# The convolution's input projection in wide pairs, with part of its elementwise work moved to ScalarE and GpSimd

## What is computed

```python
def short_conv_mixer(h, w_in, conv_w, w_out):
    """y = W_out( B * conv_w3( C * u ) ), [B, C, u] = W_in h; causal depthwise conv."""
    b_gate, c_gate, u = jnp.split(h @ w_in, 3, axis=-1)
    v = c_gate * u
    vp = jnp.pad(v, ((0, 0), (CONV_WIDTH - 1, 0), (0, 0)))
    conv = sum(conv_w[k] * vp[:, k:k + S] for k in range(CONV_WIDTH))
    return (b_gate * conv) @ w_out
```

## Time and profile before

| | us |
|---|---|
| median of 3 runs | 1196.76 (1193.81 to 1199.23) |
| the profiled execution | 1195.6 |
| its span, first to last instruction | 1193.8 |
| outside the span | 1.8 |
| TensorE busy | 1184.0, 99% |
| VectorE busy | 859.2, 72% |
| ScalarE busy | 644.1, 54% |
| GpSimd busy | 226.9, 19% |
| mean granted TensorE clock | 0.997 of full |

### The profile page before, as it was taken

The page is one execution under the profiler, slowest core; times in us unless marked ns, Lnnn a source line. Parts: engine busy times, 40 slices in busy tenths (PEclk is TensorE's granted clock), DMA queues, the critical chain, the costliest instruction groups (busy, mean ns, idle before and its releaser), DMA issues.

```text
span 1193.8 us, 19183 instructions
## 1 busy us (share of the span) xinstructions
PE 1184.0 (99%) x7641; PEld 1055.1 (88%) x7641; DVE 859.2 (72%) x1178; ACT 644.1 (54%) x860; POOL 226.9 (19%) x115
## 2 busy tenths in 40 slices
PE   9999999999999999999999999999999999999997
PEld 6888889988899888888999988888899978888886
DVE  6877767788868877766788786656578777766353
ACT  6655454465655755544643455444446784555432
POOL 1443301000000334310000024520000250455001
PEclk9999999999999999999999999999999999999999
DMA  8655555953245554555545555555576305555550
GB/s 319 212 180 198 186 177 187 275 209 107 106 151 180 178 208 177 194 194 182 177 161 186 187 204 206 179 197 192 181 278 233 121 19 177 186 202 178 184 202 36
DMA packets 31567, 218.03 MB, mean 183 GB/s; under 512 B 3584, under 2 KB 3856, under 8 KB 6272
## 3 DMA queue, kind: packets, MB, share of 16 engines
q1 hardware_dynamic: 29712, 210.07, 50.2%
q0 software_dynamic: 1488, 6.05, 1.8%
q10 hardware_dynamic: 288, 0.79, 0.2%
HBM read 215.82 MB, written 4.22 MB: 184 GB/s over the span
## 4 chain that ended last, share of the span: by engine, by line
PE 93%; DVE 4%; DMA 2%; ACT 1%; issue 1%; SPq 0%; DVEq 0%; ACTq 0%
PE bank L1634 38%; PE bank L1635 19%; PE bank L1627 7%; PE bank L1628 7%; PE bank L1629 7%; PE bank L1826 2%; PE bank L1825 2%; PE bank L1824 2%; DVE w_hl L858 1%; DMA raw<-weights 1%; PE bank L2081 1%; ACT w_hl L438 1%; PE bank L1975 0%; DMA par<-small 0%; PE bank L1755 0%
## 5 line engine op out<-in xcount | busy, mean ns | idle before, releaser
L858 DVE TENSOR_TENSOR w_hl<-raw,w_hl 128x2048 fp32r<-128x2048 f32 x194 | 444.0, 2289 | 134.1 <-ACT w_hl L438 133.2
L438 ACT ACTIVATE w_hl<-raw 128x2048 fp32r<-128x2048 f32 x195 | 370.5, 1902 | 135.8 <-PE bank L1635 46.6
L1634 PE MATMUL bank<-x_hl,w_hl 128*128 128x512 f32 x905 | 315.2, 394 | 0.2 <-DVE w_hl L1077 0.2
L377 POOL TENSOR_TENSOR hidden<-hid_f,hidden 128x256 fp32r<-128x256 f32 (+1 forms) x76 | 189.6, 2494 | 517.7 <-ACT hidden L521 306.0
L1635 PE MATMUL bank<-x_hl,w_hl 128*128 128x256 f32 x905 | 251.9, 278 | 0.0
L1634 PE MATMUL bank<-hidden,w_hl 128*128 128x512 f32 x608 | 210.9, 393 | 0.0
L1634 PEld LDWEIGHTS bank<-x_hl,w_hl 128*128 128x128 f32 x905 | 169.6, 187 | 39.1 <-DVE x_hl L908 0.7
L1635 PEld LDWEIGHTS bank<-x_hl,w_hl 128*128 128x128 f32 x905 | 170.4, 188 | 0.2
L1635 PE MATMUL bank<-hidden,w_hl 128*128 128x256 f32 x608 | 169.0, 278 | 0.0
L1634 PE MATMUL bank<-y_hl,w_hl 128*128 128x512 f32 x445 | 155.3, 395 | 0.0
L1627 PE MATMUL bank<-x_hl,w_hl 128*128 128x256 f32 x528 | 151.2, 286 | 0.1
(11 more groups left out here) (397 smaller groups left out, 1713.6 us busy)
## 6 DMA issues: line engine op xcount, KB each, us to landing
raw<-weights SPq DMA_DIRECT2D x197, 1024.0 KB, 4.9
bias_skew<-bias_rows POOLq DMA_DIRECT2D x1, 3072.0 KB, 28.6
gate_or_bias<-bias_skew POOLq DMA_DIRECT2D x1, 2048.0 KB, 10.3
h<-x_t SPq DMA_DIRECT2D x2, 512.0 KB, 5.6
con<-consts SPq DMA_DIRECT2D x1, 769.5 KB, 12.7
raw<-weights ACTq DMA_DIRECT2D x1, 512.0 KB, 5.1
raw<-weights SPq DMA_DIRECT2D x1, 512.0 KB, 7.5
sv<-last_gain POOLq DMA_DIRECT2D x1, 512.0 KB, 4.0
```

The lines of the kernel that those rows point to most:

```text
L377: nc.gpsimd.tensor_tensor(hidden[:, at, 1, :], src, hidden[:, at, 0, :].bitcast(F32), ALU.subtract).then_inc(hid_lo, 1)
L438: nc.scalar.activation(dst, src, ACT.Copy).then_inc(hi_split, 1)
L858: V.tensor_tensor(w_lo[:, s, :], raw[:, s, :], w_hi[:, s, :].bitcast(F32), ALU.subtract).then_inc(lo_split, 1)
L1634: mm(out_, w_hi[:, s, c:c + m], x, start=start, stop=False, **kw)
```

## The change

The product of conv_in is now done by `wide`, chunk j of a turn on banks 0 and 1, 2 and 3, or 4 and 5 (one bank for each tile of 128 features). ScalarE copies the second halves of both banks to SBUF (`conv_half`), VectorE adds the first halves to them (`whole`, into t_ab) and goes on from t_ab. The factor of the norm, which VectorE multiplied to B, is multiplied to the sum of the taps by GpSimd, as soon as the last tap is there. The low part of y is made by GpSimd too. VectorE's y_f waits for GpSimd's product (`taps_scaled`). In conv_out, the one place where a low product stood ahead of the wide one is now in the plain order; in conv_in, where there was none, one is added.

```diff
--- before.py
+++ after.py
@@ -93,6 +93,7 @@
 
 ACC, TURN, SUMS = 0, 4, 7
 OUT_BANKS = ((0, 1), (2, 1), (6, 1), (0, 0))
+CONV_BANKS = ((0, 1), (2, 1), (4, 1))
 NSA_OUT_BANKS = ((3, 1), (6, 1), (0, 1), (2, 0))
 HID = {"ffn1": 0, "ffn2": FF, "mlp0": 2 * FF, "mlp1": 2 * FF + MF}
 UPS = {"ffn1": FF, "ffn2": FF, "mlp0": MF, "mlp1": MF}
@@ -213,6 +214,7 @@
         dve_step, act_step = sem("dve_step"), sem("act_step")
         ab_ready, sum_ready, r_ready, rt_mm, conv_full = (
             sem("ab_ready"), sem("sum_ready"), sem("r_ready"), sem("rt_mm"), sem("conv_full"))
+        conv_second, taps_done, taps_scaled = sem("conv_second"), sem("taps_done"), sem("taps_scaled")
         rope_ang, rope_sin = sem("rope_ang"), sem("rope_sin")
         sv_done, qk_raw, ss_head = sem("sv_done"), sem("qk_raw"), sem("ss_head")
         rq_mm, rq_done = sem("rq_mm"), sem("rq_done")
@@ -393,6 +395,12 @@
             pool.dma_start(heads[:, 0:2, :], p_t).then_inc(p_in, 16)
             pool.wait_ge(p_in, 16)
             low("ffn2")
+            for i in range(4):
+                pool.wait_ge(taps_done, i + 1)
+                nc.gpsimd.tensor_tensor(hid_f[:, :, :], hid_f[:, :, :], r_two, ALU.mult).then_inc(taps_scaled, 1)
+                pool.wait_ge(op_hi, PC["conv"] + i + 1)
+                nc.gpsimd.tensor_tensor(y_l[:, 2 * i:2 * i + 2, :], y_f[:, 2 * i:2 * i + 2, :],
+                                        y_h[:, 2 * i:2 * i + 2, :].bitcast(F32), ALU.subtract).then_inc(op_lo, 1)
             low("mlp0")
             pool.wait_ge(chunk_used, C["mlp0"] + 2 * MF)
 
@@ -720,13 +728,24 @@
             nxt(PLE_GATE[3])
             nc.scalar.preload_act_table_set("natural_log_exp_and_others")
             c0 = C["conv_in"]
+
+            def conv_half(i, j):
+                act.wait_ge(chunk_used, i * 3 + (c0 + j + 1))
+                if j != 1:
+                    act.wait_ge(drained, i * 3 + (DRAIN["conv"] + j // 2))
+                nc.scalar.activation(second[:, j % 2, :, :], halves(CONV_BANKS[j], 1), ACT.Copy).then_inc(conv_second, 1)
+
+            conv_half(0, 0)
             nxt(c0)
             rsqrt("mix0", load=False)
 
             def conv_turn(i):
                 if not isinstance(i, int):
+                    conv_half(i, 0)
                     nxt_in(c0, 0, i, 3)
+                conv_half(i, 1)
                 nxt_in(c0, 1, i, 3)
+                conv_half(i, 2)
                 act.wait_ge(conv_full, i + 1)
                 nc.scalar.activation(y_h[:, bass.ds(i * 2, 2), :], y_f[:, bass.ds(i * 2, 2), :], ACT.Copy).then_inc(op_hi, 1)
                 nxt_in(c0, 2, i, 3)
@@ -1316,39 +1335,43 @@
 
             def conv_turn(i):
 
-                st.n = i * 8 + n
+                def whole(j):
+                    dve.wait_ge(conv_second, i * 3 + (j + 1))
+                    V.tensor_tensor(t_ab[:, :, :], halves(CONV_BANKS[j], 0), second[:, j % 2, :, :],
+                                    ALU.add).then_inc(drained, 1)
+                    dve.wait_ge(drained, i * 3 + (DRAIN["conv"] + j + 1))
+
+                st.n = i * 9 + n
                 for j in range(2):
-                    dve.wait_ge(chunk_used, i * 3 + (c0 + j + 1))
-                    st.done(V.tensor_tensor(t_ab[:, j, :], bank[:, TURN + j, 0:S], t_m[:, :], ALU.mult))
-                    V.tensor_tensor(v_pad[:, j, 2:S + 2], t_ab[:, j, :], bank[:, TURN + j, S:2 * S],
-                                    ALU.mult).then_inc(drained, 1)
-                    dve.wait_ge(drained, i * 3 + (DRAIN["conv"] + j + 1))
+                    whole(j)
+                    st.done(V.tensor_tensor(t_ab[:, 0, :], t_ab[:, 0, :], t_m[:, :], ALU.mult))
+                    st.done(V.tensor_tensor(v_pad[:, j, 2:S + 2], t_ab[:, 0, :], t_ab[:, 1, :], ALU.mult))
                     for k in range(3):
                         tap = 2 - k
                         w = par[:, bass.ds(i * 2 + (SM["conv_w"] + 8 * tap + j), 1)]
                         src = v_pad[:, j, tap:tap + S]
                         if k == 0:
                             st.done(V.tensor_scalar(hid_f[:, j, :], src, w, None, ALU.mult))
+                            continue
+                        ins = V.scalar_tensor_tensor(out=hid_f[:, j, :], in0=src, scalar=w, in1=hid_f[:, j, :],
+                                                     op0=ALU.mult, op1=ALU.add)
+                        if j == 1 and k == 2:
+                            ins.then_inc(taps_done, 1)
                         else:
-                            st.done(V.scalar_tensor_tensor(out=hid_f[:, j, :], in0=src, scalar=w,
-                                                           in1=hid_f[:, j, :], op0=ALU.mult, op1=ALU.add))
+                            st.done(ins)
                     if j == 1 or not isinstance(i, int):
                         nxt_in(c0, j, i, 3)
-                dve.wait_ge(chunk_used, i * 3 + (c0 + 3))
-                V.tensor_tensor(t_ab[:, :, :], two(bank[:, TURN + 2, :]), r_two, ALU.mult).then_inc(drained, 1)
-                dve.wait_ge(drained, i * 3 + (DRAIN["conv"] + 3))
+                whole(2)
+                dve.wait_ge(taps_scaled, i + 1)
                 V.tensor_tensor(y_f[:, bass.ds(i * 2, 2), :], t_ab[:, :, :], hid_f[:, :, :],
                                 ALU.mult).then_inc(conv_full, 1)
-                dve.wait_ge(op_hi, i + (PC["conv"] + 1))
-                V.tensor_tensor(y_l[:, bass.ds(i * 2, 2), :], y_f[:, bass.ds(i * 2, 2), :],
-                                y_h[:, bass.ds(i * 2, 2), :].bitcast(F32), ALU.subtract).then_inc(op_lo, 1)
                 nxt_in(c0, 2, i, 3)
 
 
             conv_turn(0)
             with dve.Fori(1, 4) as i:
                 conv_turn(i)
-            st.n = n + 32
+            st.n = n + 36
             made[0] += 4
 
             project_out("conv_out", "mlp0", x_h, x_l)
@@ -1694,7 +1717,7 @@
                                 pe.wait_ge(op_lo, PC[pieces] + p + 1)
                             for t in range(2):
                                 for k in range(KT // n * p, KT // n * (p + 1)):
-                                    if j == 0 and t == 0 and k == 1 and banks[j][1] > 0:
+                                    if j == 0 and t == 0 and k == 1 and pieces != "conv":
                                         last = wide_low_first(bank[:, banks[j][0], :], c % RING, 256, P, x[:, 1, :, :])
                                         continue
                                     last = out_tile(banks[j], (c + j) % RING, t, k, x, k == 0, k == KT - 1)
@@ -2037,14 +2060,14 @@
 
 
             c = C["conv_in"]
-            two_pairs(c, ((TURN, 0), (TURN + 1, 0)), x_hl, "mix0", 3, between=lambda: sum_squares(7))
+            two_pairs(c, CONV_BANKS, x_hl, "mix0", 3, between=lambda: sum_squares(7))
             arrived(c + 3)
-            pair((c + 2) % RING, TURN + 2, x_hl).then_inc(chunk_used, 1)
+            out_chunk(CONV_BANKS[2], (c + 2) % RING, x_hl)
             with pe.Fori(1, 4) as i:
                 for j in range(3):
                     arrived(i * 3 + (c + j + 1))
                     pe.wait_ge(drained, i * 3 + (DRAIN["conv"] + j - 2))
-                    pair((c + j) % RING, TURN + j, x_hl).then_inc(chunk_used, 1)
+                    out_chunk(CONV_BANKS[j], (c + j) % RING, x_hl)
             c = C["conv_out"]
             two_pairs(c, OUT_BANKS, y_hl, "conv", 3)
             for j in range(2, 4):
```

## The result

| | before | after |
|---|---|---|
| median, us | 1196.72 (11 runs) | 1203.2 (11 runs) |
| ratio of the runs | | 1.0054 [1.0042, 1.0066] |
| a second set beside the experiments | 1197.64 (26 runs) | 1203.49 (9 runs), 1.0050 [1.0031, 1.0069] |
| span of the profiled execution | 1193.8 | 1203.5 |
| conv_in's first matmul to mlp0's first, "stage time" below | 92.31 | 97.66 |

What follows compares the result with a forecast made beforehand. VectorE's turn of 18.3 takes the bound from TensorE's 16.65: splits slip +1.46, +0.57, 1.89 a loop turn, to +7.21 at chunk 13; TensorE starts it +5.4 later, giving 1202.2, range 1198.5 to 1206.3.

Steps and rivals of the forecast that it cites:

- VectorE is only 0.9 faster than TensorE, and it starts late: In conv_in before the change: VectorE's turn takes 16.42, TensorE's 17.28, and TensorE starts chunk 5 only 0.13 after its split.
- Sum of halves: New VectorE work in conv_in for j = 0 and 1: +1.44 a turn, upper bound +1.66; for j = 2 zero.
- the last tap no longer holds up the split: On VectorE in conv_in, gives back 0.05 in the first turn and about 0.1 in the loop.
- GpSimd's product: Norm factor on the taps' sum runs behind VectorE's split, ending 1.14 later: y_f +0.49 a turn, +0.57 in the first.
- Low part of y: Moving it off VectorE in conv_in saves nothing, since it lay inside the wait for ScalarE.
- The sum: Delays of VectorE's splits in conv_in add to +7.21 for chunk 13, so TensorE starts that chunk +5.4 later.
- two ties: Near conv_in's end, y's last low part and chunk 14's split are ready about when TensorE is: up to 0.5 if one slips.
- TensorE's pace: Rival: TensorE sets the pace in conv_in and its gain comes through, -2.6, 1194.2; chance 0.08.
- GpSimd not held up: Rival: GpSimd's product ends while VectorE's split runs, only the sums of halves count, +3.9, 1200.6; chance 0.12.
- GpSimd first: Rival: GpSimd's product starts first and VectorE's split for j = 1 waits about 1.14, +8.5, 1205.3; chance 0.12.

Runs made afterwards that it cites:

- e2: The kernel before with the wide pairs alone, second halves read by nobody and no sums of halves: stage time 90.79, ratio 0.9995.
- e3: The changed kernel with ScalarE making the next weights' high part ahead of y's at a turn's end: stage time 92.89, ratio 1.0000.
- e5: The kernel before with only ScalarE's swap, the weights' high part ahead of y's: stage time 91.96, ratio 0.9992.
- e1: The changed kernel without GpSimd's product of the taps' sum with the norm factor: stage time 96.13, ratio 1.0029.
- e7: The changed kernel with VectorE's sum of halves for j = 2 ahead of the split for j = 1: stage time 98.56, ratio 1.0071.
- e8: e4 with y's high part behind the next turn's first half copy and weights, chunk 14's split behind the last low part: stage time 92.58, ratio 1.0004.
- e6: The changed kernel with the low part of y back on VectorE: stage time 97.70, ratio 1.0050.
- e4: e3 with VectorE's splits in the first turn one place earlier: stage time 92.48, ratio 1.0003.

## Why the prediction was right

**What bounds.** The step "VectorE is only 0.9 faster than TensorE, and it starts late" carried the forecast. e2 shows the late start by itself (0.8 of TensorE's 2.6 lost), e3 and e5 that VectorE's chain is what bound after and not before.

**Sum of halves.** Forecast +1.44 a turn with 0.83 each as the upper bound. Measured, distance of its start to the next instruction 0.73 in the first turn (619.10 to 619.83) and 0.71 to 0.72 in the loop: right, at the forecast value. What was mis-sized is the term beside it: that the last tap no longer holds up the split gives back 0.2 in a loop turn (the split now starts 0.08 before the tap's end, before 0.13 after it), not 0.1. From the turn's start to the split for j = 1 the loop is 1.25 longer (11.24 against 9.99), where the sum had 1.4.

**GpSimd's product.** Forecast 3.53 from split to y_f, measured 3.53 in the first turn (625.13 to 628.66) and 3.58 in the loop; product ending 1.14 after the split, measured 1.14. Of the three rows at hand (0.89, 1.14, 1.30) the one with two full inputs was the right one. e1 confirms its price, e7 the mechanism from the other side. The rule of the Trainium skill (SBUF — State Buffer, "SBUF: two separate sides"), first come holds the ports, agrees with both. e8 adds that VectorE's tensor_scalar can be the one that waits (1.14 against 0.35). The Trainium skill (SBUF — State Buffer, "Who interferes with whom") has this for tensor_scalar in its two-port modes; whether the tap ran in such a mode is not shown by any row.

**Low part of y.** Forecast zero; e6 has 97.70 against 97.66.

**Start and end of the stage.** The sum was +5.4 at chunk 13. Measured from conv_in's start, chunk 13 is at 681.77 - 602.70 = 79.07 after, and before at 674.07 - 599.99 = 74.08:

```profile
674.07 0.39 PE L1634 MATMUL bank<-y_hl,w_hl 128*128 128x512 f32 x1
```

So it is +5.0 there and not +5.4. The splits say where: that for chunk 5 is 2.10 later than before (forecast 2.03), for chunk 8 3.88 (3.92), for chunk 11 5.67 (5.81), for chunk 13 6.90 (7.21). In VectorE's timeline after, the last two are

```profile
668.23 2.29 DVE L877 TENSOR_TENSOR w_hl<-raw,w_hl 128x2048 fp32r<-128x2048 f32 x1 [2.69 <-ACT w_hl L446]
...
679.43 2.28 DVE L877 TENSOR_TENSOR w_hl<-raw,w_hl 128x2048 fp32r<-128x2048 f32 x1
```

The loop's turns came out at 18.20 and 18.17 instead of 18.31, and the last stretch short by as much again, by the tap's term above. Behind chunk 13 the stage takes 18.59 to mlp0 against 18.23. The forecast had two ties there, up to 0.5 if one slipped, but neither did: the last low part of y ends at 685.92, 0.2 before TensorE needs it, the split for chunk 14 at 688.67, 0.3 before, and TensorE's rows show no wait. The 0.36 is TensorE's own: 36 pairs there 0.3532 apart against 0.347 (0.24), and 0.1 for the late second matmul behind the wait, told of at the end. So that the stage's +5.35 falls on the forecast's +5.4 is in part luck: the chain was 0.4 over, and a term that the forecast did not have gave nearly that back.

**The rivals.** TensorE's pace (-2.6) fell: TensorE loses 6.15 us to waits in the stage. GpSimd not held up fell by the 3.27. GpSimd first fell for this kernel, by 0.16 us of order.

**Size and chance.** +6.5 [5.0, 7.9] by the medians holds the stage's +5.35. The prediction had 0.40 for slower by over 0.5% and 0.56 for within; measured are 1.0054 [1.0042, 1.0066] and 1.0050 [1.0031, 1.0069], so on which side of 0.5% the change lies can't be told.

## What to carry to other kernels

Where one engine is 99% busy, look how far ahead of it its suppliers are, chunk by chunk: a gain there is worth no more than their lead, and here a supplier with 28% idle time had a lead of 0.2 us at chunk 4 and none at chunk 5. In a chain with cross-engine waits, look first at the order of the queue that stands in it (here ScalarE's, 4.8 us of the changed kernel by one swap), and then at moving work off the engine (0.0 for the low part of y, minus 1.5 for the product). Here that took back the loss and no more: no version measured is faster than the kernel before by more than the runs can tell. Work handed to GpSimd while VectorE runs an operation with two SBUF inputs can stand until that ends: here 1.29 of work took 3.27 and ended 1.14 after the split.

## What the runs showed that I had not expected

TensorE's wide pairs have two distances, with the same instructions, no wait and full granted clock: 0.3467 and 0.3533 on the mean, 2% apart. An execution keeps one of them for long. In ffn1, from 38 us to its end near 195, it is the short one before and the long one after: TensorE's timelines, before and after, over three pairs,

```profile
99.86 0.39 PE L1634 MATMUL bank<-x_hl,w_hl 128*128 128x512 f32 x1
...
100.90 0.39 PE L1634 MATMUL bank<-x_hl,w_hl 128*128 128x512 f32 x1
```

```profile
99.94 0.40 PE L1657 MATMUL bank<-x_hl,w_hl 128*128 128x512 f32 x1
...
101.00 0.40 PE L1657 MATMUL bank<-x_hl,w_hl 128*128 128x512 f32 x1
```

1.04 for three pairs against 1.06. Of eleven profiles five have the long distance in ffn1 (after, its repeat, e3, e4, e7), one also in mlp0, and in those five conv_in starts at 602.7 to 604.0, in the other six at 599.8 to 600.5. The instructions ahead of it are the same in all. A chunk costs 0.1 more at the long distance. In conv_in it can also change on the way, at a wait or between two chunks: e2 has the short distance throughout (0.3467), e3 and e8 the long one from chunk 3 on, e4 the long one from there to its wait before chunk 6 and the short one behind it, and the changed kernel mostly the long one (its repeat mostly the short one). Twelve chunks at the long distance are 1.2, near half of the 2.6 that wide pairs can win there, so stage times of single profiles that differ by less than that are not told apart by them where TensorE is the bound. In the profiles ffn1 at the long distance goes with a start of conv_in about 3 us later; it may well be part of why single runs of one kernel lie 5 us apart here, but the runs without a profile don't show it. What sets a stage into one or the other stays open; no run here was made for it.

Behind a wait for the split the first pair also starts its second matmul late: 0.33 after the first instead of 0.24 (627.55 to 627.88 at chunk 4 of the changed kernel), 0.1 for each chunk that is waited for.
